# Cached value pages of a sampling step: eight visits of two batches in a group in place of sixteen of one

## What is computed

```python
h = _rmsnorm(x, g_pre) * (1 + scale[:, None]) + shift[:, None]
p = h @ w_in
hc, bc, cc, gc, q, k, v, ga = jnp.split(p, _split_points(), axis=-1)
...
ya = _rmsnorm(bc * conv_y, g_conv) * jax.nn.silu(gc)
o = attend(q, k, v, b_sb).reshape(Bsz, L, ATT_DIM)
yb = _rmsnorm(o, g_attn) * jax.nn.silu(ga)
m = jnp.concatenate([ya, yb], axis=-1) @ w_out
y = x + gate[:, None] * _rmsnorm(m, g_post)
```

```python
past_k = pool_k[page_table].reshape(Bd, past, H, Dh)
past_v = pool_v[page_table].reshape(Bd, past, H, Dh)
...
a = jnp.where(mask, jnp.exp(jax.nn.log_sigmoid(z) + after), 0.0)
return jnp.einsum('bhqk,bkhd->bqhd', a.astype(v.dtype), v)
```

## Time and profile before

| | |
|---|---|
| median of 3 runs | 833.01 us (830.09 to 834.65) |
| profiled execution, span from first to last instruction | 830.7 us |
| PE busy | 788.8 us, 95% |
| DVE, POOL, ACT busy | 541.9, 429.6, 349.9 us |
| queue of SP and ACT transfers (q1) | 181.11 MB, 66.1% of 16 engines' span |
| mean granted TensorE clock | 0.990 |

### The profile page before, as it was taken

How to read it: one execution, slowest core, us unless ns; L and a number is a source line. 1 busy time by engine, 2 the same in 40 slices (tenths; PEclk the granted TensorE clock), 3 DMA queues, 4 the chain that set the end, 5 groups by cost and what they waited for, 6 DMA issues and landing times.

```text
span 830.7 us, 14505 instructions
## 1 busy us (share of the span) xinstructions
PE 788.8 (95%) x4445; PEld 520.1 (63%) x4445; DVE 541.9 (65%) x739; ACT 349.9 (42%) x722; POOL 429.6 (52%) x230
## 2 busy tenths in 40 slices
PE   0889989999999999999999999999999999999995
PEld 0455866676877566668866766778676665433442
DVE  2575779787575688847749886586788854232344
ACT  7301065774122557821155676122658731122122
POOL 0105895575786556666966485687665630100000
PEclk9989999999999999999999999999999999999999
DMA  8998777677689867876898886878977797555001
GB/s 317 362 347 283 223 227 226 201 230 245 219 242 323 270 222 255 253 250 207 285 299 266 246 259 206 280 227 286 304 243 245 230 346 286 156 182 172 27 26 53
DMA packets 131071, 197.85 MB, mean 238 GB/s; under 512 B 10025, under 2 KB 51030, under 8 KB 130994
## 3 DMA queue, kind: packets, MB, share of 16 engines
q1 hardware_dynamic: 99512, 181.11, 66.1%
q10 hardware_dynamic: 31482, 15.82, 6.8%
HBM read 185.25 MB, written 11.66 MB: 237 GB/s over the span
## 4 chain that ended last, share of the span: by engine, by line
PE 76%; DVE 6%; issue 6%; POOL 4%; DMA 4%; SPq 2%; ACT 1%; POOLq 0%; DVEq 0%; ACTq 0%
PE ps L1356 72%; PE ps L1600 4%; POOL prod L614 3%; DMA xT<-in_x_prompt_dram 2%; DMA ring<-in_w_in_dram 1%; DVE zd L1210 1%; DVE ps L1234 1%; SPq L383 1%; DMA ring<-in_cache_k_dram 1%; DVE xT L1014 1%; DVE zc L1240 1%; DVE zc L1220 1%; SPq L375 0%; PE ps L1398 0%; POOL wsl L597 0%
## 5 line engine op out<-in xcount | busy, mean ns | idle before, releaser
L614 POOL TENSOR_TENSOR prod<-ring,qb 128x1024 f32<-128x1024 f32 x128 | 308.8, 2428 | 201.3 <-DMA ring<-in_cache_k_dram 90.0
L1356 PE MATMUL ps<-hT,wsl 128*128 128x258 f32 (+1 forms) x640 | 174.4, 418 | 0.1
L1210 DVE TENSOR_REDUCE zd<-prod 128x16 f32<-128x1024 f32 x128 | 154.3, 1212 | 29.1 <-POOL prod L614 28.6
L1356 PEld LDWEIGHTS ps<-hT,wsl 128*128 128x128 f32 x640 | 118.9, 190 | 54.3 <-issue 19.6
L1356 PE MATMUL ps<-xT,wS 128*128 128x258 f32 x352 | 92.2, 385 | 0.0
L1356 PE MATMUL ps<-xT,wsl 128*128 128x258 f32 x352 | 90.1, 387 | 0.0
L1356 PE MATMUL ps<-ring,apad 128*8 128x512 f32 (+1 forms) x592 | 79.7, 618 | 7.4 <-DMA ring<-in_w_ada_dram 6.8
L1220 DVE TENSOR_SCALAR zc<-ps,bsb 128x512 f32<-128x512 f32 (+3 forms) x96 | 54.8, 612 | 42.6 <-PE ps L1356 42.2
L654 ACT ACTIVATE rise<-ps,bsh 128x512 f32<-128x512 f32 (+3 forms) x96 | 55.4, 577 | 49.9 <-DVE zc L1220 49.7
L1356 PEld LDWEIGHTS ps<-xT,wsl 128*128 128x128 f32 x352 | 63.1, 190 | 19.7 <-issue 8.7
L654 ACT ACTIVATE av<-ps 128x512 f32<-128x512 f32 (+3 forms) x96 | 46.7, 487 | 63.1 <-PE ps L1600 61.9
(11 more groups left out here) (241 smaller groups left out, 1021.0 us busy)
## 6 DMA issues: line engine op xcount, KB each, us to landing
ring<-in_cache_k_dram SPq DMA_DIRECT2D x256, 256.0 KB, 3.6
ring<-in_cache_v_dram SPq DMA_DIRECT2D x256, 256.0 KB, 3.1
wsl<-in_w_in_dram ACTq DMA_DIRECT2D x30, 512.0 KB, 6.6
ring<-in_w_ada_dram SPq DMA_DIRECT2D x5, 2048.0 KB, 15.1
xT<-in_x_prompt_dram SPq DMA_DIRECT2D x2, 2048.0 KB, 10.9
out_dram<-oT SPq DMA_DIRECT2D x8, 512.0 KB, 4.6
ring<-in_x_prompt_dram SPq DMA_DIRECT2D x8, 512.0 KB, 6.4
xT<-y_parts SPq DMA_DIRECT2D x6, 512.0 KB, 9.5
```

Source lines behind the costliest of these rows:

```text
L614: pool.tensor_tensor(prod[:, p % 2].rearrange("p (j c) -> p j c", j=2), kring[:, p % 4], qb[:, p // 16].unsqueeze(1).to_broadcast([P, 2, H ...
L1210: v.tensor_reduce(zd[:, t // 16, :, r:r + 2], prod[:, t % 2].rearrange("p (j h d) -> p h j d", j=2, h=NH), AX_X, ALU.add)\
L1356: return nc.tensor.matmul(out, l, r, start=start, stop=stop, skip_group_check=True)
```

## The change

Two batches of a sample stand in one slot, one behind the other. The slots become 1, 5, 8, 12 for sample 2g - 1 and 20, 24, 28, 32 for sample 2g. SP requests the four pairs of both batches together, at the place in its list of the slot two before. At the end of a group it requests batches 0 and 1 of the next sample, where it requested batch 0. The waits for free places in the ring stay one per batch.

```diff
-def quad_of(slot):
-
-    for parity, slots in ((1, (0, 3, 6, 8, 10, 12, 14, 16)), (0, (20, 22, 24, 26, 28, 30, 32, 33))):
+def quads_of(slot):
+
+    for parity, slots in ((1, (1, 5, 8, 12)), (0, (20, 24, 28, 32))):
         if slot in slots:
-            return parity, slots.index(slot)
-    return 0, None
+            at = 2 * slots.index(slot)
+            return parity, (at, at + 1)
+    return 0, ()
...
             def load_quad(g, first, t):
 
-                parity, quad = quad_of(t)
-                if quad is not None and not (first and parity == 1):
+                parity, quads = quads_of(t)
+                if first and parity == 1:
+                    return
+                for quad in quads:
                     for rr in (2 * quad, 2 * quad + 1):
                         load_v(2 * g - parity, rr, None if first and quad < 2 else 16 * g - 8 * parity + quad - 1)
...
                 if not last:
-                    for rr in range(2):
-                        load_v(2 * g + 1, rr, 16 * g + 7)
+                    for rr in range(4):
+                        load_v(2 * g + 1, rr, 16 * g + 7 + rr // 2)
...
                 def page_values(t):
-                    parity, quad = quad_of(t)
-                    if quad is None or (first and parity == 1):
+                    parity, quads = quads_of(t)
+                    if first and parity == 1:
                         return
-                    value_quad(2 * g - parity, quad)
+                    for quad in quads:
+                        value_quad(2 * g - parity, quad)
```

## The result

The changed kernel takes **851.98 us** (median of 4 runs, 850.0 to 853.94), the kernel before on the same chip 831.98 (4 runs, 830.09 to 834.65): a ratio of **1.0252**, 95% interval 1.0225 to 1.028 (the two medians divided give 1.0240; all ratios below are formed as the first one). It is slower, as forecast, and inside the range; the forecast was 844.0. The profiled execution has a span of 848.9 us against 830.7, +18.2 where the sum said +11.0. The mean granted clock is 0.989.

What follows compares the result with a forecast made beforehand. The prediction took TensorE (PE), busy 95% of the span, as the bound. Terms of 9.1 and 1.9 us gave 11.0 on a span of 830.7; with the median 2.3 above the span, 844.0, range 832 to 856.

Steps and rivals of the forecast that it cites:

- Part 1: PE's visits of value batches: each pair saves 0.13 us, 28 pairs 3.6 us (bounds 0 and 14).
- Part 3: Slots 0 to 13, groups 1 to 3: K pair 16 requested late, behind all eight value batches; with slot shifts +9.1 us.
- like their mean: Group 3, slot 8's visit to the turn of unit 4: counted as 17.6 us before, so a delay of 3.3.
- Part 4: Slot 22, all four groups: K pair 25 requested behind four V pairs, not two; +0.48 us per group, +1.9 in all.
- part 2: Slots losing a visit lose cover: wait 1.43 us for 0.44 after slot 14, about 0.6 at slot 30, nothing at 26.
- The K pages are not late: Rival: SP runs ahead or landings shorten, so savings and lost cover give +0.1 us, 833.1, no change; chance 0.18.
- pure gain: Rival: only fewer drains, and slot 13's waits and the half clock go too, 825 us; chance 0.07.
- slower still: Rival: K25 lands as late as before (+6.8), lower clock in groups 2 and 3 (1.5 us each), 853.8; chance 0.25.

Runs made afterwards that it cites:

- f_num_after: The changed kernel with SP reading eight page numbers, for four pairs, in one table load instead of two per pair; 843.9 us, 1.0178 against the kernel before.
- f_slot0: The changed kernel with the odd sequence's first pair of batches moved from slot 1 to slot 0; 850.8 us, ratio 1.0243 against the kernel before.
- g_num0: The changed kernel with eight page numbers per table load and the odd sequence's first pair in slot 0; 840.1 us, 1.0117 against the kernel before.

## Why the prediction was right, and where its sizes were off

The direction, the range and the large term came as told; the sum was 7.2 us short in the profile. Slots 20 to 32 were short by 5.2 and slots 32 to 19 by 2.3, each summed over the groups; the two ends gave 0.4 back.

**Part 1, PE's own time: right.** A pair takes 1.85 us from its start to the next instruction. PE in order of time, group 3, slot 8:

```profile
591.32 1.91 PE L1359 MATMUL ps<-ring,apad 128*8 128x512 f32 x16
593.17 2.01 PE L1359 MATMUL ps<-hT,wsl 128*128 128x258 f32 x8
```

**Part 3, SP's queue: right that it is the large term, too narrow in its path.** f_num_after takes part of SP's time away, and of the 8.5 us in slots 32 to 19 it takes 6.4 (the same edit takes 2.5 to 2.7 off the kernel before). K16's request came 11.5, 10.9 and 11.9 us behind slot 8's visit in groups 1 to 3 for 11.0, the turn of unit 4 at 21.7, 20.2 and 21.9 for 20.9. The step that was too narrow is that K16 alone sets the end. K13, K14 and K15 of group 2, requested 2.1 to 2.3 us apart, landed 4.7, 6.3 and 7.1 us after their requests (4.5, 4.4 and 6.5 before; why K14 and K15 took longer is open). So waits came in slots 9 to 11 as well. PE, group 1, slot 10, and group 3, slots 9, 10 and 13:

```profile
274.35 0.47 PE L1604 MATMUL ps<-ident,zc 128*128 128x128 f32 x1 [2.56 <-DVE zc L1243]
...
598.24 0.33 PE L1604 MATMUL ps<-ident,zc 128*128 128x128 f32 x1 [1.75 <-DVE zc L1243]
...
601.96 0.33 PE L1604 MATMUL ps<-ident,zc 128*128 128x128 f32 x1 [1.14 <-DVE zc L1243]
...
613.25 0.49 PE L1604 MATMUL ps<-ident,zc 128*128 128x128 f32 x3
```

Only in group 2 does PE still wait at the turn of unit 4. In group 1 its log weights are ready just in time, and in group 3 at 612.72, 0.53 us ahead: there K13 to K15 set the end, and K16 costs nothing. That group, taken "like their mean", grew by 4.25 in place of 2.05. SP was later there ahead of K13:

```profile
584.16 0.43 SPq L439 DMA_DIRECT2D y_parts<-gab  x1
588.14 5.04 SPq L384 DMA_DIRECT2D ring<-in_cache_k_dram  x6
```

The table load between the two took 2.49 us, 1.28 in group 2 and 0.47 at the median of all. So K13 went out 3.2 us ahead of slot 8's visit, 5.0 and 4.7 in groups 1 and 2 (forecast 4.0). The prediction had taken SP's time per pair as fixed and y_parts as 2.76 in every group.

**Part 4, K25: the request right, its effect in another place.** In group 3 K25 went out 9.92 us behind slot 20's visit (9.58 forecast), its product began at 14.7 (14.3). The sum let half of the 0.8 us vanish in slack. It did not: part 2 had said of slot 26 that "nothing is lost here", and looked only at the turn of unit 18. Ahead of that turn, in slot 26, stands a product that waits for VectorE's sum (L1094), and that sum queues behind the late reductions of K25 and K26. PE, group 3, slots 24, 26 and 31:

```profile
653.88 0.29 PE L1359 MATMUL ps<-ident_b,unseen 128*128 128x128 bf16 x2 [0.20 <-ACT av L657]
...
665.02 0.70 PE L1359 MATMUL ps<-xT,wsl 128*128 128x258 f32 x2 [1.15 <-DVE ub L1094]
...
685.63 0.66 PE L1604 MATMUL ps<-ident,zc 128*128 128x128 f32 x4 [0.76 <-DVE zc L1243]
```

With K25 in time (f_num_after) this wait is gone and slots 19 to 32 grow by 1.98 per group in place of 2.78 on average: K25 cost 0.8, for 0.4 forecast. The rest of the miss is 0.4 at slot 24 (0.20 of it the wait for av), 0.3 at slot 30 (0.93 for 0.6; 0.76 is the wait) and 0.2 at slot 26; in each of these a little under 0.2 us is left that no wait names. Over four groups the term was 5.2 us short.

**Part 2, cover: right at slots 14 and 30.** Slot 14's visit bought nothing: in group 2 the turn of slot 14 comes 0.99 earlier against slot 13's, and that of slot 15 0.99 later against slot 14's, than before. Its wait is 0.98, not 1.43; a wait of 0.18 for zb ahead of it (455.01) has a part of the rest. Not seen was slot 0: there the visit had covered ACT's copy of vN. It costs 0.78 us of wait in each of groups 1 to 3, and up to slot 8's visit the growth is 0.36 for -0.26. These three times 0.6, 1.6 between that visit and the turn of unit 4 (+0.7, -0.6 and +1.5) and -1.1 behind it make the 2.3 us by which slots 32 to 19 were short.

**The rivals.** "The K pages are not late" and "pure gain" fell. Of "slower still", K25's part did not come (its request to product took 4.6, 4.4, 5.2 and 4.8 us in groups 0 to 3, in one group past the 5 from which it decides and nowhere near 6.45), and neither did the lower clock of groups 2 and 3: PE runs at 0.54 from 274 to 277 us of group 1, as in the kernel before, and at 1.00 from 433 to 442 and from 598 to 607. Its total, 853.8, came nearer than the forecast's 844.0 all the same, by other waits, which is chance.

```profile
274.00:277.00 3.00, 2.65 (x8) 1.99 (x9) 2.13 (x4) 2.20 (x7) 3.00 (x2) 0.54 0.95 308
277.00:280.00 3.00, 3.00 (x16) 2.42 (x16) 2.21 (x5) 1.78 (x7) 1.99 (x3) 0.89 1.00 284
```

(Columns as in the earlier trace rows.) The Trainium skill says in "DMA: Bandwidth & Descriptors", Issuing engines are not separate DMA queues, that the sequencer time to initiate a DMA is usually small relative to the DMA itself. This trace agrees as far as the requests go: the two of a pair take 0.85 us of SP, against 3.6 us to landing of a K page; the prediction had set SP's whole 2.08 us against that sentence. What weighed here is the reading of the page numbers ahead of them, about 1.2 us per pair: making that cheaper, and nothing else, took some 6 us off the changed kernel's ratio and 10.4 us off its profile.

## What to carry to other kernels

Where an engine's small pieces of work stand between waits, they are cover: moving two of them together moves their time to a place where it adds, and leaves a hole where the wait comes up. Before merging, look in each slot that loses work at every instruction there that waits for another engine, the copies and sums too, and not only at the wait that the list shows today. Requests merged for the sake of one consumer stand in one queue with those of others: count the issuing engine's own time per request, the reading of addresses included, and if it decides, make the requests cheaper before changing their order.

## What the runs showed that I had not expected

- Cheaper requests land later. With SP's time for eight V requests down from 7.42 to 3.95 us, the median from request to landing rose from 3.1 to 4.2 us for V and from 3.6 to 4.5 for K. With its load of numbers a pair costs SP 2.08 us before and about 1.7 now ((3.95 + 2.8) / 4), so 0.4 us less, and lands about 1 us later. What is still won adds up over the pairs in the queue: in group 2 K13 is requested 10.0 us ahead of slot 8's visit in place of 4.7.
- Moving a wait of 0.78 us out of the way gave nothing in one kernel (f_slot0) and 2.6 us in the profile of another (g_num0), where the three waits had been 2.3 in all.
- The lower clock behind a long wait is short, and not every long wait brings it. Behind PE's wait of 3.11 us in f_slot0 the granted clock is 0.51 from 598 to 601 us and 0.92 from 601 to 604. Behind a wait of 2.04 us in the same kernel (slot 10 of group 2, to 435.90) it stays at 1.00 from 435 to 441, where the kernel before has 0.50 behind one of 1.96. So a longer wait does not bring the lower clock of itself, as one of the rivals had it.
